# Neighbourhood attention in a two block kernel: where the last value product runs, how scores use PE and PSUM, and how values are turned

## What is computed

```python
q = rms_norm_2(q, g_q); k = rms_norm_2(k, g_k)      # 16 heads of d = 32
# rows of 64 columns; a block is 16 query columns, its keys 32 columns of 8 rows
kb = np.minimum(cs[:, 0], GRID_W - K_COLS)          # 0, 8, 24, 32
sc = jnp.einsum('bjqhd,bjkhd->bhjqk', qb, kg) * scale + bias
pr = jax.nn.softmax(sc, axis=-1)
o = jnp.einsum('bhjqk,bjkhd->bjqhd', pr, vg)
...
h = h + jnp.concatenate([oa, ob], axis=-1) @ w_out[i]
```

## Time and profile before

| what | us |
|---|---|
| median of the three runs | 1571.65 |
| the profiled execution, first to last instruction | 1566.4 |
| PE busy in it | 1521.5 |
| DVE busy | 717.2 |
| ACT busy | 530.1 |
| POOL busy | 165.2 |
| differential attention, PE's first to last scores | 778.6 to 880.8 |
| neighbourhood attention, PE's first scores to the next stage | 893.7 to 976.9 |

### The profile page before, as it was taken

One profiled execution on the slowest core, in us unless ns is written; L12 is line 12 of the kernel. 1 busy time (PEld: TensorE's weight loads), 2 busy tenths in 40 slices (PEclk: granted clock), 3 DMA queues, 4 the chain that ended last, 5 costly groups with the idle time before them and its releaser, 6 DMA issues.

```text
span 1566.4 us, 19659 instructions
## 1 busy us (share of the span) xinstructions
PE 1521.5 (97%) x7812; PEld 1062.6 (68%) x7812; DVE 717.2 (46%) x1208; ACT 530.1 (34%) x910; POOL 165.2 (11%) x171
## 2 busy tenths in 40 slices
PE   6999999999999999999999989999999999999998
PEld 6766788898888888888777766745444444444366
DVE  5336333365444544478665788531132132132174
ACT  5334422355232432345455577431011011010042
POOL 0024100002110211111300210011000000000000
PEclk9999999999999999999999999999999999999999
DMA  7111432313222222222110232879999999999951
GB/s 276 54 55 62 175 105 83 121 68 107 82 108 108 100 87 83 108 95 83 53 54 28 84 133 105 330 303 400 418 421 421 421 420 421 421 421 421 421 239 55
DMA packets 45437, 311.22 MB, mean 199 GB/s; under 512 B 5136, under 2 KB 5648, under 8 KB 10016
## 3 DMA queue, kind: packets, MB, share of 16 engines
q1 hardware_dynamic: 42480, 296.74, 47.6%
q0 software_dynamic: 2864, 13.19, 2.3%
HBM read 301.52 MB, written 8.39 MB: 198 GB/s over the span
## 4 chain that ended last, share of the span: by engine, by line
PE 88%; DVE 5%; ACT 3%; issue 2%; DMA 1%; SPq 0%; DVEq 0%; ACTq 0%
PE bank L798 21%; PE bank L2492 14%; PE bank L2508 7%; PE bank L1416 7%; PE bank L833 6%; PE bank L2475 4%; PE bank L2525 4%; PE bank L850 4%; PE bank L2691 3%; PE bank L1273 3%; PE bank L811 2%; PE bank L821 2%; PE bank L868 1%; PE bank L842 1%; DVE M L2123 1%
## 5 line engine op out<-in xcount | busy, mean ns | idle before, releaser
L622 DVE TENSOR_TENSOR w_lo<-M,w_hi 128x2048 fp32r<-128x2048 f32 x73 | 169.8, 2331 | 182.1 <-ACT w_hi L617 182.1
L2492 PE MATMUL bank<-M 128*64 128x512 f32 x1024 | 226.8, 595 | 0.0
L617 ACT ACTIVATE w_hi<-M 128x2048 fp32r<-128x2048 f32 x73 | 139.1, 1912 | 146.4 <-PE bank L798 56.9
L798 PE MATMUL bank<-HTH,w_hi 128*128 128x512 f32 x432 | 168.1, 389 | 0.0
L798 PE MATMUL bank<-HTL,w_hi 128*128 128x512 f32 x432 | 168.1, 389 | 0.0
L798 PE MATMUL bank<-HTH,w_lo 128*128 128x512 f32 x432 | 168.1, 389 | 0.0
L2492 PEld LDWEIGHTS bank<-M 128*64 128x64 f32 x1024 | 70.7, 137 | 135.5 <-issue 134.4
L2508 PE MATMUL bank<-M 128*64 128x512 f32 x512 | 113.6, 595 | 1.4 <-DMA M<-in_w 1.3
L2650 DVE TENSOR_TENSOR X<-bank,X 128x512 f32<-128x512 f32 x69 | 46.5, 688 | 109.7 <-PE bank L2525 109.6
L798 PEld LDWEIGHTS bank<-HTH,w_lo 128*128 128x128 f32 x432 | 81.1, 188 | 17.0
L798 PEld LDWEIGHTS bank<-HTH,w_hi 128*128 128x128 f32 x432 | 81.1, 188 | 16.8
(11 more groups left out here) (373 smaller groups left out, 2834.3 us busy)
## 6 DMA issues: line engine op xcount, KB each, us to landing
M<-in_w SPq DMA_DIRECT2D x192, 1024.0 KB, 11.1
M<-in_wd SPq DMA_DIRECT2D x78, 1024.0 KB, 4.8
...
```

The costliest lines, as they stand in the source:

```text
L617: e.activation(hi[:, :], slots[slot_of[n]], ACT.Copy).then_inc(split_hi_done, 1)
L622: e.tensor_tensor(lo[:, :], slots[slot_of[n]], hi[:, :], ALU.subtract).then_inc(split_lo_done, 1)
L798: m = e.matmul(out[:, :], w[:, k0 + k, n0:n0 + 128], v[k], start=(k == 0 and i == 0), stop=(k == len(hi) - 1 and i == 2))
L2492: m = e.matmul(b[64 * s:64 * s + 64, :], Xe[:, 4 * kh + k, o + C * s:o + C * s + C], unit_w(key, 4)[:, k, :], start=(kh == 0 and k == 0), ...
```

## The change

- Of the value product only `vb` 0 and 1 stay woven into the differential steps, and from step 8 on a step takes at most one woven half. `vb` 2 and 3 run as four halves in neighbour steps 0 to 3 (`VB_AT`); DVE evacuates 2 in step 2 and ACT evacuates 3 in step 4. The split of the last input weight moves from differential step 11 to 13.
- Scores: one matmul of 32 rows for each head, into its own bank (0 to 3) in columns 0 to 255. QM, POOL's spreading and its semaphore are deleted; the queries are put into block order when ACT evacuates them, in two instructions a tile instead of one.
- Values are turned group by group, in steps 0, 2, 6 and 10 (`VJ_AT`), two transposes to columns 256 to 511 of each score bank; ACT evacuates two of the four, DVE the other two.
- `oa` 2 and 3 move from steps 0 and 2 to 4 and 5; outputs 0 and 1 get buffers of their own (OAH, OAL). The pieces of `o2a` start in step 6 instead of 4 and end in step 17 instead of 18. Weight splits of the output product stand in steps 3, 9, 14 and 16 instead of 2, 12, 15 and 16.
- Transposes of probabilities use banks 7 and 5 (first steps 7 and 6, 7 and 4) instead of rotating over 0, 5 and 3; the value product has bank 6 alone instead of 6 and 7.
- The first neighbour bias has its own place and its load waits for the turned queries; the first load into the spare slot waits for the end of the neighbour steps instead of nothing.

The diff, without context, some renamings and deleted calls left out:

```diff
@@ -174,6 +174,8 @@
+        OAH = [overlay(f"OAH{i}", R0 + 2048 + 512 * i, NTOK) for i in range(2)] + [HTH[:, i, :] for i in (2, 3)]
+        OAL = [overlay(f"OAL{i}", R0 + 3072 + 512 * i, NTOK) for i in range(2)] + [HTL[:, i, :] for i in (2, 3)]
@@ -344,13 +346,13 @@
-        WOVEN = [(("h", 2 + n // 4, n % 4), j) for n in range(8) for j in range(2)] + [(("vb", f), j) for f in range(4) for j in range(2)]
-        woven_by = [min(len(WOVEN), (3 * i + 4) // 2) for i in range(len(DIF) + 3)]
+        WOVEN = [(("h", 2 + n // 4, n % 4), j) for n in range(8) for j in range(2)] + [(("vb", f), j) for f in range(2) for j in range(2)]
+        woven_by = [min(len(WOVEN), (3 * i + 4) // 2, i + 5) for i in range(len(DIF) + 3)]
...
-        SPLIT_AT = {5: 6, 8: 7, 11: 8}
+        SPLIT_AT = {5: 6, 8: 7, 13: 8}
@@ -370,39 +372,39 @@
-                for hp in range(2):
-                    ps.put(("ns", 0, hp), [1 + hp])
+                for hh in range(4):
+                    ps.put(("ns", 0, hh), [hh])
...
-        OA_AT = {0: 2, 2: 3}
-        VJ_AT = {0: range(0, 4), 1: range(4, 8)}
-        VJ_FIRST, VJ_ACT, VJ_DVE = (0, 1), {0: (4, 5, 6)}, {0: (2,), 2: (3, 7)}
-        O2A_IN = ((4, 5), (6, 7), (8, 9), (11, 12), (14, 15), (16, 16), (17, 17), (18, 18))
+        OA_AT, VJ_AT = {4: 2, 5: 3}, {0: 0, 2: 1, 6: 2, 10: 3}
+        VB_AT = {0: (2, 0), 1: (2, 1), 2: (3, 0), 3: (3, 1)}
+        O2A_IN = ((6, 6), (7, 8), (9, 9), (10, 11), (12, 13), (14, 14), (15, 16), (17, 17))
...
-        nt_turn = itertools.cycle((0, 5, 3))
-        NBR_BANKS = {"vj": (4, 0, 3, 6, 4, 0, 5, 3), "oa": {2: 7, 3: 4}, "ns": (1, 2), "nt": ((0, 5), (3, 7)),
-                     "o2a": (4, 4, 4, 4, 4, 1, 2, 4)}
+        O2A_BANKS = (4, 4, 4, 4, 4, 4, 4, 0)
...
-                for hp in range(2):
-                    ps.put(("ns", i, hp), [NBR_BANKS["ns"][hp]])
-            for v in VJ_AT.get(i, ()):
-                ps.put(("vj", v), [NBR_BANKS["vj"][v]])
+                for hh in range(4):
+                    ps.put(("ns", i, hh), [hh])
+            if i in VJ_AT:
+                for q in range(4):
+                    ps.put(("vj", VJ_AT[i], q), [q])
+            if i in VB_AT and VB_AT[i][1] == 0:
+                ps.put(("vb", VB_AT[i][0]), [4 + i // 2])
...
-                ps.put(("oa", OA_AT[i]), [NBR_BANKS["oa"][OA_AT[i]]])
+                ps.put(("oa", OA_AT[i]), [4])
...
-                    ps.put(("o2a", t, h), [NBR_BANKS["o2a"][t + 4 * h]])
-            if i >= 3 and (i - 3) % 4 == 0:
-                ps.put(("no", (i - 3) // 4), [6 + (i - 3) // 4 % 2], counted=False)
+                    ps.put(("o2a", t, h), [O2A_BANKS[t + 4 * h]])
...
-                    ps.put(("nt", i - 2, half), [NBR_BANKS["nt"][i - 2][half] if i < 4 else next(nt_turn)])
-        out2_banks = [1, 2, 6, 0, 5, 3, 4, 7]
+                    ps.put(("nt", i - 2, half), [(7, {2: 6, 3: 4}.get(i, 5))[half]])
+            if i >= 3 and (i - 3) % 4 == 0:
+                ps.put(("no", (i - 3) // 4), [6], counted=False)
+        out2_banks = [1, 2, 3, 5, 7, 0, 4, 6]
@@ -525,7 +527,7 @@
-        open_slots = deque([(SPARE_SLOT, "free")] + [(slot_of[n], n) for n in (NDENSE - 2, NDENSE - 1)] + [(i, "nbr") for i in (2, 3, 9, 11, 6)]
+        open_slots = deque([(SPARE_SLOT, "nbr")] + [(slot_of[n], n) for n in (NDENSE - 2, NDENSE - 1)] + [(i, "nbr") for i in (2, 3, 9, 11, 6)]
@@ -855,8 +857,8 @@
-                for i, src in enumerate((HTH,) if low else (HTH, HTL)):
-                    m = e.matmul(out[:, :], src[:, k, t * 128:(t + 1) * 128], w[:, k, :], start=(low == k == i == 0),
+                for i, src in enumerate((OAH,) if low else (OAH, OAL)):
+                    m = e.matmul(out[:, :], src[k][:, t * 128:(t + 1) * 128], w[:, k, :], start=(low == k == i == 0),
@@ -1527,14 +1529,15 @@
-        QB = [region(12288 + 512 * i, 512) for i in range(3)] + [rowb[:, 512 * i:512 * i + 512] for i in range(2)]
+        QB = [region(o, 512) for o in (12288, 12800, 16448)] + [rowb[:, 512 * i:512 * i + 512] for i in range(2)]
...
-        vbJ, Vj = mem(SPL[0], 4, 4, 256), mem(SPL[1], 8, 512)
+        Vj = mem(SPL[1], 8, 512)
+        vbJ = [mem(o, 4, 256) for o in (SPL[0], SPL[0] + 1024, R0, R0 + 1024)]
@@ -1614,6 +1617,12 @@
+            if G == 2:
+                for r in range(2):
+                    a = e.activation(qbT.rearrange("p k (j r c) -> p k j r c", j=4, c=16)[:, :, :, 2 * t + r, :],
+                                     b[:, :].rearrange("p (k r j c) -> p k r j c", k=4, r=2, c=16)[:, :, r, :, :], ACT.Copy, scale=scale)
+                a.then_inc(empties, 1)
+                return
@@ -1724,7 +1733,7 @@
-                yield vbJ[:, key[1], j, :].rearrange("p (r c) -> p r c", c=32), b4[:, :, KB[j]:KB[j] + 32], j == 3, empties
+                yield vbJ[key[1]][:, j, :].rearrange("p (r c) -> p r c", c=32), b4[:, :, KB[j]:KB[j] + 32], j == 3, empties
@@ -1765,8 +1774,7 @@
-        QM = [region(2048 * i, 4, 512) for i in range(2)]
-        NB = [mem(SPL[2], 4, 3, 256), mem(2 * UNIT, 4, 3, 256)]
+        NB = [region(13376, 4, 3, 256), mem(2 * UNIT, 4, 3, 256)]
@@ -1777,25 +1785,8 @@
-            unit_read(e, ("in2", 11))
+            filled(e, ("ht", 2, 3))
...
-        def spread(e, hg):
-            for hh in range(4):
-                src = qbT[32 * hh:32 * hh + 32, hg, :].rearrange("p (r j c) -> p j r c", j=4, c=16)
-                dst = QM[hg % 2][32 * hh:32 * hh + 32, hh, :].rearrange("p (j r c) -> p j r c", j=4, c=16)
-                e.tensor_copy(dst, src).then_inc(q_spread, 1)
-            e.wait_ge(q_spread, 4 * hg + 4)
...
-        def dif_pool(e):
-            for s in range(2):
-                filled(e, ("ds", len(DIF) - 1, s))
-            for t in range(TT):
-                taken(e, ("ht", 2, t))
-            for hg in range(2):
-                pool_own.mark(e.memset(QM[hg], 0.0))
-                e.wait_ge(pool_own.sem, pool_own.n)
-                spread(e, hg)
@@ -1866,14 +1857,15 @@
+                e.wait_ge(gs_done, 1)
+            if h == 2:
...
-                e.wait_ge(gs_done, 1)
-            e.activation(HTH[:, h, :], b[:, :], ACT.Copy, scale=gs_).then_inc(o_hi, 1)
+            e.activation(OAH[h][:, :], b[:, :], ACT.Copy, scale=gs_).then_inc(o_hi, 1)
...
-            e.scalar_tensor_tensor(out=HTL[:, h, :], in0=b[:, :], scalar=gs_, in1=HTH[:, h, :], op0=ALU.mult,
+            e.scalar_tensor_tensor(out=OAL[h][:, :], in0=b[:, :], scalar=gs_, in1=OAH[h][:, :], op0=ALU.mult,
@@ -1917,8 +1909,7 @@
-                    for v in VJ_FIRST:
-                        evac_act(e, Vj[:, v, :], ("vj", v))
+                    vj_act(e, 0)
@@ -1981,7 +1972,7 @@
-        N_PT = [spare[:, 0:D].rearrange("p (a b) -> p a b", a=8), region(10240, 8, 128)]
+        N_PT = [spare[:, 0:D].rearrange("p (a b) -> p a b", a=8), region(16960, 8, 128)]
@@ -1991,44 +1982,54 @@
-                for hp in range(2):
-                    taken(e, ("ns", 4 * hg - 5, hp))
+                for hh in range(4):
+                    taken(e, ("ns", 4 * hg - 5, hh))
...
-        def nbr_pool(e):
-            for hg in (2, 3):
-                for hp in range(2):
-                    filled(e, ("ns", 4 * hg - 5, hp))
-                spread(e, hg)
...
-            e.wait_ge(q_spread, 4 * hg + 4)
...
+                    taken(e, ("ht", 2, t))
...
-            both = [claim(e, ("ns", i, hp)) for hp in range(2)]
-            for s in range(2):
-                for hp, (b, fills) in enumerate(both):
-                    half = slice(64 * hp, 64 * hp + 64)
-                    m = e.matmul(b[:, s * 256:s * 256 + 256], QM[hg % 2][half, 2 * hp + s, 128 * j:128 * j + 128],
-                                 k4[half, hg, :, KB[j]:KB[j] + 32], start=True, stop=True)
-                    if s:
-                        m.then_inc(fills, 1)
+            for hh in range(4):
+                b, fills = claim(e, ("ns", i, hh))
+                at = slice(32 * hh, 32 * hh + 32)
+                e.matmul(b[:, 0:256], qbT[at, hg, 128 * j:128 * j + 128], k4[at, hg, :, KB[j]:KB[j] + 32], start=True,
+                         stop=True).then_inc(fills, 1)
...
+        def vj_pe(e, f):
+            taken(e, ("vb", f))
+            for q in range(4):
+                b, fills = claim(e, ("vj", f, q))
+                for n in range(2):
+                    m = e.transpose(b[:, 256 + n * 128:384 + n * 128], vbJ[f][:, q, n * 128:(n + 1) * 128], ident)
+                m.then_inc(fills, 1)
...
+        def vj_parts(e, f, q):
+            b, empties = filled(e, ("vj", f, q))
+            return Vj[:, 2 * q:2 * q + 2, f * 128:(f + 1) * 128], b[:, 256:512].rearrange("p (v n) -> p v n", v=2), empties
...
+        def vj_act(e, f):
+            for q in range(2):
+                dst, src, empties = vj_parts(e, f, q)
+                e.activation(dst, src, ACT.Copy).then_inc(empties, 1)
...
+        def vj_dve(e, f):
+            for q in range(2, 4):
+                dst, src, empties = vj_parts(e, f, q)
```

(52 more changed lines are left out.)

15 lines of the change are left out of this document (5 added, 10 removed).

## The result

| | median of the runs, us | profiled execution: span, us | first neighbour scores | neighbour stage | from there to the end |
|---|---|---|---|---|---|
| before | 1571.08 (6 runs, 1568.39 to 1571.81) | 1566.4 | 893.69 | 83.25 | 589.4 |
| after | 1575.14 (6 runs, 1574.04 to 1578.07) | 1576.3 | 886.71 | 98.09 | 591.5 |

The ratio is 1.0039, 95% interval 1.0028 to 1.0051: the change makes the kernel slower by 0.4%, some 6 us. The neighbour stage is counted here from its first score row on TensorE (PE) to the first product of the next stage. The two profiled executions are 9.9 us apart, the medians only 4.1. Before's was about 3 us faster than its own median: its span of 1566.4 and the 1.8 us or so that lie around a span give 1568.2. After's was about 3 us slower than its own (1578.07). So a difference of single traces has to be read by places, and its sum not taken for the time.

What follows compares the result with a forecast made beforehand. PE was taken as the bound, without gaps in the differential steps, with a DVE and ACT round setting the first neighbour steps. Differential -6.8 and neighbour +8.9 give +2.1; 1566.4 + 2.1 + 5.2 = 1573.8 us, range 1564 to 1580.

Steps and rivals of the forecast that it cites:

- rival B: Neighbour and late differential steps: longer PE idle stretches bring 1.2 GHz clock, 1.7 us each, up to +5: 1578.8; chance 0.25.
- Part 1: Differential steps: four half products leave, gain 9.9 us; step 13 piles up, loss 3.1; sum 6.8 us earlier.
- Part 2: Neighbour scores on PE: 32-row matmuls side by side take 0.63 us a step instead of 1.06, saving 0.43.
- the upper end: Neighbour scores: 1.06 us a step, if no more than two matmuls overlap.
- rival C: Neighbour scores: the four row groups do not overlap, 0.43 us in each of nine late steps, +3.9: 1577.7; chance 0.10.
- Part 3: Neighbour steps: step 7 starts at 42.35 us after the first scores instead of 32.9; whole stage 8.9 us longer.
- The walk: Neighbour steps followed in order with a price for each operation, giving block starts and PE waits, 4.7 us in step 4.
- Steps 7 to 18: Late neighbour steps: 43.9 us of PE work and 5.9 of waits, 49.8 instead of 50.4.
- Part 4: Query evacuations, neighbour bias load and first expert loads: edits at nothing; ends for the expert loads 0 and +1 us.
- The total: Whole kernel: -6.8 + 8.9 = +2.1 us on the profiled span of 1566.4, plus 5.2 around the span: 1573.8 us.
- Rival A: Neighbour steps 4 and 5: rounds don't add up, half products fill idle PE, stage keeps 83.3 us: 1564.9; chance 0.20.

Runs made afterwards that it cites:

- x8_samerow: Changed kernel with all four score matmuls of a step reading the same 32 rows, so none can overlap; 1591.25 us, ratio 1.0132.
- x2_vb3: Changed kernel with ACT's copy of value product 3 ahead of the exponentials of neighbour step 4 instead of behind them; 1575.15 us, ratio 1.0036.
- x4_spare: Kernel before with only the first expert weight load made to wait for the end of the neighbour steps; 1569.59 us beside 1569.32, ratio 1.0001.
- x7_both: Changed kernel with value transposes behind the step's product and the ACT and DVE round of neighbour steps 2 to 5 reordered; 1562.32 us, ratio 0.9955.
- x6_round: Changed kernel with only the ACT and DVE round of neighbour steps 2 to 5 reordered (output parts, value copy, weight split earlier); 1567.01 us, ratio 0.9987.

## Why the prediction was right, point by point

The time was right (1573.8 for 1575.14), the direction too, though the nearness of the time is in part luck, as the total below shows. In the profiled execution it is rival B's mechanism that makes most of what the forecast lacks. Step by step:

- **Part 1, differential stage 6.8 us earlier.** Measured 6.98 (893.69 to 886.71), of which 0.57 was there before step 8 (829.98 after, 830.55 before) and isn't the change's: 6.4 remain. Step 13 starts at 856.85 (forecast 857.5), the steps before it take 5.35 to 5.41 each, and step 15 comes 13.55 us after it (14.2), behind a 2.81 us wait for ACT (870.40). The long scaling on DVE, 997 ns beside POOL's copies, has 490 as its maximum now that POOL does nothing there. The undisturbed DVE times were the right ones to use.
- **Part 2, scores 0.63 us.** Measured 0.64 to the next PE start, from the row of its own kind. The Trainium skill (TensorEngine Tiling (Array Packing), Performance Considerations) has four tiles for a contraction of 32; 1.92 us in one row group against 0.64 in four agrees, at a factor of 3. That evacuation may then become the limit agrees for the early steps: the longest waits of PE there are for banks that ACT and DVE have yet to read. But the overlap isn't worth little: x8_samerow is 15 us slower. It was the upper end that was mis-sized, and with it the price of rival C.
- **Part 3, up to step 7: forecast 42.35, measured 47.46.** The distances from block to block are right but for three: step 1 to 2 is 2.3 us too long, 4 to 5 1.5, and 6 to PE's step 7 1.1. The walk had the right waits, with the right releasers (4.68 us for the bank of product 3 where 4.7 was forecast, ACT's high part ahead of its copy, DVE's split behind the low part). The term that failed is the one left out of the sum: the clock, 4.2 of the missing 5.1 us. It was priced nearly right, at 1.7 us a stretch, though without a row for the price (1.6 measured in step 1), and kept as a rival, though the earlier trace rows showed a clock of 0.91 just behind idle stretches, and the walk had found longer ones. The four falls of after come behind waits of 2.34 us (ahead of 878.82, for DVE), 1.20, 4.68 and 1.97 us. Not every wait brings one: x2_vb3 has 1.21 us in step 1, too, and no fall behind it. The Trainium skill (TensorE: Matmul & The Clock Gate, HAM oscillation — how this bites in real kernels) asks for a PE without long idle gaps for the sake of the clock; the trace agrees in direction, but falls came behind shorter waits too (1.20 and 1.97 us). The waits of about 3 us that rival B asked for were not needed.
- **Steps 7 to 18: 49.8 forecast, 50.63 measured,** with the 1.64 and 0.80 us waits between output products as walked. The parts are further off than the sum: PE is busy 45.60 us and idle 5.0, where the walk had 43.9 of work and 5.9 of waits (its three waits add up to 5.8, and the start of step 7 to 42.24 instead of 42.35; neither matters).
- **Part 4.** Nothing at the queries and the bias load, as forecast. The expert loads are issued as forecast, and the waits at the end grew by 1.8 us in the trace of after. x4_spare gives 1.4 in its trace and no time. The forecast of 0 to 1 is neither confirmed nor refuted.
- **The total.** By traces the sum should have been -7.0 + 14.8 + 2.1 = 9.9, and the forecast had 2.1. That 1573.8 came near nonetheless has a reason that isn't merit: 5.2 us were added as lying around the span, but only 1.6 to 2.2 do, in every run. The other 3.4 were the distance of before's profiled execution from its median. With 1.8, the same walk gives 1570.3, since it starts from an execution that happened to be fast. The right base was the median of the kernel before, 1571.65 then: plus 2.1 that is 1573.7. The medians differ by 4.1, so 1.4 us were missing (2.0 from the later median of 1571.08). The falls that the change adds are the likely reason: its mean clock is 0.992 to 0.994, where the kernel before has medians of 0.996 to 0.997. No run shows their share in a median execution by itself.
- **Rival A** (rounds that don't add up, the half products filling idle PE time) is refuted for the kernel as written. x7_both comes near what it described: the stage 84.5 us, where A had 83.3, and the time 1562.3, where A had 1564.9. It needed another order on three engines.
- **Rival B** held in mechanism: the clock makes 4.2 of the 6.0 us by which the stage of the profiled execution is longer than forecast, where B had up to 5. In the median only 1.4 to 2.0 us are missing, so its share there is likely smaller. **Rival C** is refuted by the row of 0.64 us and by x8_samerow.

Whether the time could be had back by holding the clock up through such waits stays open: with fillers the mean clock rose, and the time gained nothing clear. The trace of x7_both alone had no fall in the stage. Its longest PE waits there are 1.64 and 1.37 us, but that isn't the whole reason: x6_round, whose waits are no longer, had one fall.
